# Second block's output projection: the attention half of its input turned early, first halves of all four tiles run around the recurrence's head norm

## What is computed

```python
def mixer_ab(h, w_in, lb, hg_norm, w_out):
    ...
    o_a = stick_breaking_attention(qa.reshape(sb_shape), ka.reshape(sb_shape), va.reshape(sb_shape))
    o_a = o_a.astype(h.dtype).reshape(B, S, SB_WIDTH)
    o_b = hgrn2(qb.reshape(B, S, HG_HEADS, HG_DK), fb.reshape(B, S, HG_HEADS, HG_DK), ib.reshape(B, S, HG_HEADS, HG_DV), lb)
    o_b = rmsnorm_2(o_b.astype(h.dtype), hg_norm) * jax.nn.silu(gb.reshape(B, S, HG_HEADS, HG_DV))
    o_b = o_b.reshape(B, S, HG_V)
    return jnp.concatenate([o_a, o_b], axis=-1) @ w_out
...
            h = h + mixer_ab(hn, ab_w_in[j], lower_bounds[j], hg_out_norm[j], ab_w_out[j])
...
        h = h + conv_glu_ffn(rmsnorm_2(h, ffn_norm[i]), ffn_up[i], ffn_conv[i], ffn_conv_b[i], ffn_down[i])
```

## Time and profile before

| | before |
|---|---|
| median of 3 runs (lowest to highest) | 1537.84 us (1537.67 to 1540.51) |
| span of the profiled execution | 1536.3 us |
| its own time with what lies around the span | not given apart; the median is 1.5 us over the span |
| TensorE busy | 1381.1 us (90%) |
| VectorE busy | 1029.5 us (67%) |
| ScalarE busy | 710.5 us (46%) |
| GpSimd busy | 568.9 us (37%) |
| mean granted TensorE clock | 0.973 |

### The profile page before, as it was taken

How to read it: one execution, slowest core, us unless ns; L and a number is a source line. 1 busy time by engine, 2 the same in 40 slices (tenths; PEclk the granted TensorE clock), 3 DMA queues, 4 the chain that set the end, 5 groups by cost and what they waited for, 6 DMA issues and landing times.

```text
span 1536.3 us, 18265 instructions
## 1 busy us (share of the span) xinstructions
PE 1381.1 (90%) x6001; PEld 969.0 (63%) x6001; DVE 1029.5 (67%) x1917; ACT 710.5 (46%) x1377; POOL 568.9 (37%) x541
## 2 busy tenths in 40 slices
PE   7999998778777887777779999999999999999998
PEld 6887963323333333333336878788888778888887
DVE  4885787666666666666655548659863686498734
ACT  5545453222333332233324463477645655776534
POOL 3040454333333333333344422055433512364414
PEclk9999999998998999999899999999999999999999
DMA  9295699999999999999998510567665443476650
GB/s 315 91 179 189 247 385 422 421 421 422 422 421 422 420 423 422 421 422 422 422 421 312 192 48 13 165 184 203 191 216 194 158 140 92 134 207 195 214 188 28
DMA packets 180739, 414.99 MB, mean 270 GB/s; under 512 B 9178, under 2 KB 113218, under 8 KB 148418
## 3 DMA queue, kind: packets, MB, share of 16 engines
q0 software_dynamic: 37440, 268.45, 42.1%
q1 hardware_dynamic: 143090, 145.66, 30.9%
q10 hardware_dynamic: 144, 0.04, 0.0%
HBM read 409.93 MB, written 4.19 MB: 270 GB/s over the span
## 4 chain that ended last, share of the span: by engine, by line
PE 52%; DMA 23%; DVE 9%; ACT 6%; POOL 5%; issue 4%; ACTq 0%; POOLq 0%; DVEq 0%
DMA expert_rows<-in_peer_uv,route_idx 13%; PE ps L2522 10%; DMA work_b<-in_peer_uv,route_idx 9%; PE ps L2347 8%; PE ps L2063 8%; PE ps L2065 8%; PE ps L2064 8%; PE ps L2523 5%; POOL weights_lo L588 2%; POOL expert_rows L637 2%; ACT weights_hi L433 2%; DVE weights_lo L440 2%; PE ps L2028 1%; DVE expert_rows L1645 1%; POOL ple_proj_lo L588 1%
## 5 line engine op out<-in xcount | busy, mean ns | idle before, releaser
L1645 DVE CUSTOM_DVE_ANT_0 expert_rows<-expert_rows,ps 128x1024 f32<-128x1024 f32 x180 | 219.4, 1220 | 133.9 <-DMA expert_rows<-in_peer_uv,route_idx 132.0
L2347 PE MATMUL ps<-expert_rows,proj 128*128 128x512 f32 x512 | 248.6, 644 | 63.5 <-ACT proj L952 63.5
L637 POOL DMA_INDIRECT expert_rows<-in_peer_uv,route_idx x191 | 184.5, 966 | 288.9 <-PE ps L2347 218.9
L588 POOL TENSOR_TENSOR weights_lo<-weights_raw,weights_hi 128x512 fp32r<-128x512 f32 x116 | 153.4, 1356 | 352.2 <-ACT weights_hi L433 310.3
L433 ACT CAST weights_hi<-weights_raw 128x2048 fp32r<-128x2048 f32 x98 | 185.5, 1917 | 106.3 <-PE ps L2065 82.6
L2347 PEld LDWEIGHTS ps<-expert_rows,proj 128*128 128x128 f32 x512 | 102.9, 206 | 208.4 <-issue 122.5
L2522 PE MATMUL ps<-x_normT,weights_hi 128*128 128x512 f32 x640 | 222.5, 393 | 0.0
L440 DVE TENSOR_TENSOR weights_lo<-weights_raw,weights_hi 128x2048 fp32r<-128x2048 f32 x69 | 163.1, 2370 | 61.2 <-ACT weights_hi L433 60.8
L938 ACT ACTIVATE proj<-proj 128x4 f32<-128x4 f32 x64 | 13.1, 205 | 408.0 <-DVE proj L1645 408.0
L2063 PE MATMUL ps<-weights_hi,x_normT 128*128 128x512 f32 (+1 forms) x496 | 188.2, 379 | 9.3 <-DVE weights_lo L440 3.2
L2065 PE MATMUL ps<-weights_hi,x_normT 128*128 128x512 f32 (+1 forms) x496 | 184.7, 372 | 0.0
(11 more groups left out here) (369 smaller groups left out, 2411.3 us busy)
## 6 DMA issues: line engine op xcount, KB each, us to landing
weights_raw<-in_ffn_up SPq DMA_DIRECT2D x88, 512.0 KB, 5.0
weights_raw<-in_ffn_down SPq DMA_DIRECT2D x22, 1024.0 KB, 5.0
weights_raw<-in_ab_w_in SPq DMA_DIRECT2D x14, 1024.0 KB, 5.1
weights_raw<-in_w_in SPq DMA_DIRECT2D x12, 1024.0 KB, 7.9
weights_raw<-in_ple_gate SPq DMA_DIRECT2D x8, 1024.0 KB, 6.3
weights_raw<-in_c_w_in SPq DMA_DIRECT2D x6, 1024.0 KB, 5.7
weights_raw<-in_w_out SPq DMA_DIRECT2D x4, 1024.0 KB, 12.0
weights_raw<-in_peer_w_query SPq DMA_DIRECT2D x4, 1024.0 KB, 11.9
```

The source lines that it names most:

```text
L588: ins = pool.tensor_tensor(w.lo[:, c], w.raw[:, c], w.hi[:, c].bitcast(F32), ALU.subtract)
L637: nc.gpsimd.indirect_dma_start(out=dst, out_offset=None, in_=table, in_offset=bass.IndirectOffsetOnAxis(ap=r_idx[:, q, n:n + 1], axis=0)). ...
L1645: ins = nc.vector.tensor_tensor_reduce(out=rows, in0=rows, in1=tokens, scale=1.0, scalar=0.0, op0=ALU.mult, op1=ALU.add, accum_out=r_dot[: ...
L2347: ins = pe.matmul(PS[:, (J[f"peer_{t}"] + m) % 8, :], DIAG[b][:, k, :], rows[:, m * BANK:(m + 1) * BANK], start=False, stop=False, skip_gr ...
```

## The change

- The attention half of `x_norm` is turned early: two jobs `mix1a`, between the first `spans` job and level 0, where a filler stood. ScalarE writes their high parts behind the exponentials of level 3's span (once the masked keys are done, whose place they take), VectorE the low parts behind the operands of level 1. The recurrence half follows as `mix1b` behind the head norm.
- TensorE runs the first halves of tiles (0,0) and (1,0) behind the outputs `hg_O`, turns the recurrence half, and runs the first halves of (0,1) and (1,1), then the four second halves in the old order. Fillers around them go.
- Pieces 1 and 2 of `about` change slots (0 and 2 lie in slots 0 and 1, 3 and 1 in slots 2 and 3), with new waits for the loads of 1 and 3.
- Splits: pieces 0 and 2 are cast on ScalarE ahead of the span exponentials; piece 0's low part is made on VectorE between the two copies of `sb_O`, piece 2's on GpSimd behind the masked keys. Piece 1 is cast behind the gate's silu, with its low part on VectorE where piece 0's was; piece 3 is cast behind `hg_O`, with its low part behind the low parts of `mix1b`.
- The head norm's rows, the squares and one level's operands move to other buffers.

```diff
-        ("sb_O", 2), ("hg_D", 2), ("hg_R3", 2), ("hg_L0", 2), ("hg_L1", 2), ...
+        ("sb_O", 2), ("hg_D", 2), ("hg_R3", 2), ("mix1a", 2), ("hg_L0", 2), ("hg_L1", 2), ...
-        ("mix1", 4), ("about", 3), ("norm3_0", 2), ("about_last", 1), ...
+        ("mix1b", 2), ("about", 3), ("norm3_0", 2), ("about_last", 1), ...
-        PIECES += [x for n in range(2) for x in chunk("about", n, ((0, 1), (2, 3))[n], a["ab_w_out_2"][0], 512 * n)]
+        PIECES += [x for n in range(2) for x in chunk("about", n, ((0, 3), (1, 2))[n], a["ab_w_out_2"][0], 512 * n)]
...
@@ SyncE
-            for p in halves(0):
+            for p in (0, 2):
                 load("about", p)
-            sp.wait_ge(pe_done, END["hg_L5"])
+            sp.wait_ge(pe_done, END["hg_L1"])
+            load("about", 1)
+            sp.wait_ge(pe_done, END["hg_L3"])
+            sp.wait_ge(sem("h_lev"), 12)
             sp.wait_ge(sem("h_bexp"), 1)
-            for p in halves(1):
-                load("about", p)
+            load("about", 3)
...
@@ GpSimd
             chunk_keys(hKST, hSF, 512, hKK)
-
+            split("about", 2)
             pool.wait_ge(sem("h_silu"), 2)
...
@@ ScalarE
+            for p in (0, 2):
+                split("about", p)
             for n in range(3, 6):
...
+                if n == 3:
+                    act.wait_ge(sem("kst_ready"), 6)
+                    x_hi(J["mix1a"], jobs=(0, 1))
             act.wait_ge(evac_done, END["ab_6b"])
             nc.scalar.activation(hg, hg, ACT.Silu).then_inc(sem("h_silu"), 1)
-            for p in halves(0):
-                split("about", p)
-            mixed(1, "about")
+            act.wait_ge(pe_done, END["hg_U"])
+            act.wait_ge(sem("h_lev"), 12)
+            split("about", 1)
+            sqrt_table()
+            act.wait_ge(pe_done, END["hg_O"])
+            split("about", 3)
+            root(SS[:, 16:24], SS[:, 8:16], GDV)
+            x_hi(J["mix1b"], pairs=PAIRS[2:], jobs=(0, 1))
...
@@ VectorE
             for t in range(TT):
                 j = J["sb_O"] + t
                 freed(nc.vector.tensor_copy(XN[:, t, 0:512], bank(j)), j)
+                if t == 0:
+                    split_lo(v, "about", 0)
...
             operands(0)
             operands(1)
+            x_lo(J["mix1a"], pairs=PAIRS[:2])
             mask_level(0)
...
             v.sem_inc(sem("state_ready"))
-            split_lo(v, "about", 0)
+            split_lo(v, "about", 1)
             v.wait_ge(sem("gates_gained"), 2 * TT)
-            head_norm(J["hg_O"], hg, XN[:, :, 512:1024], lambda: split_lo(v, "about", 1))
-            x_lo(J["mix1"])
-            for p in halves(1):
-                split_lo(v, "about", p)
+            head_norm(J["hg_O"], hg, XN[:, :, 512:1024], hOUTN, hSQ)
+            x_lo(J["mix1b"], pairs=PAIRS[2:])
+            split_lo(v, "about", 3)
...
@@ TensorE
             spans(3)
-            spin(J["hg_L0"], 4)
+            pe.wait_ge(evac_done, END["sb_O"])
+            mixed_T(J["mix1a"], PAIRS[:2])
             for n in range(2):
                 level(n)
...
-            mixed_T(1, END["sb_O"], 2)
-            spin(J["about"], 3)
...
-            residual_dense("about", 3, (END["mix1"], None), lambda: up_tokens(0, 0, 0), behind_norm=lambda: up_tokens(0, 1, 0))
+            dense_tile("about", 0, 0, (END["mix1a"], None), parts=(0,))
+            dense_tile("about", 1, 0, parts=(0,))
+            pe.wait_ge(sem("mixed"), TT * 2)
+            mixed_T(J["mix1b"], PAIRS[2:])
+            dense_tile("about", 0, 1, parts=(0,))
+            dense_tile("about", 1, 1, parts=(0,))
+            dense_tile("about", 0, 0, (None, END["mix1b"]), parts=(1,))
+            dense_tile("about", 1, 0, parts=(1,))
+            dense_tile("about", 0, 1, parts=(1,))
+            norm_T(3, 0)
+            dense_tile("about", 1, 1, parts=(1,))
+            up_tokens(0, 0, 0)
+            norm_T(3, 1)
+            up_tokens(0, 1, 0)
```

More of the change, by code:

```diff
@@ L41 @@
         ("ab_4", 2), ("ab_5", 1), ("sb_C", 6), ("ab_5b", 1), ("ab_6", 1), ("hg_B", 2), ("hg_T", 4), ("ab_6b", 1), ("hg_suf", 2),
[1 row of a table removed]
[1 row of a table added]
         ("hg_R5", 2), ("hg_L4", 2), ("hg_L5", 2),
         ("hg_O", 2),
-        ("mix1", 4), ("about", 3), ("norm3_0", 2), ("about_last", 1), ("norm3_1", 2), ("up0", 2 * FT),
+        ("mix1b", 2), ("about", 3), ("norm3_0", 2), ("about_last", 1), ("norm3_1", 2), ("up0", 2 * FT),
         ("down0_0", 2), ("norm4_0", 2), ("down0_1", 2), ("pT0", 1), ("gate0_first", 1), ("norm4_1", 2), ("gate0_mid", 1),
@@ L314, in build @@
         hE2 = M2[:, 1024:2048]
-        hE = (hE0, hE1, hE2, hBT, B[:, 2048:3072], A[:, 0:1024])
+        hE = (hE0, hE1, hE2, hBT, B[:, 0:1024], A[:, 0:1024])
+        hOUTN, hSQ = (A[:, n * 1024:(n + 1) * 1024].rearrange("p (t n) -> p t n", t=TT) for n in (1, 2))
         SPANS = SCR[:, 2048:2048 + 3 * P].rearrange("p (l t) -> p l t", l=3)
@@ L886, in mixed @@
                 sqrt_table()
[L887 to L891, removed]
-                    for p in halves(1):
[L893 to L897, removed]
+                root(SS[:, 16:24], SS[:, 8:16], GDV)
+                x_hi(J[f"mix{k}"], MIX_COL[k], MIX_PAIRS[k])
+                for p in halves(1):
+                    split(second, p)
             def residual_norm(k, name, between):
@@ L1423, in moba_queries, with head_norm @@
                 moba_qk(0, waiting=queries_splits)
-            def head_norm(first_job, gates, dst, between=None):
+            def head_norm(first_job, gates, dst, rows=OUTN, squares=SQ):
                 for t in range(TT):
[L1428 to L1433, removed]
+                    freed(nc.vector.tensor_copy(rows[:, t], bank(first_job + t)), first_job + t, True)
+                    step(nc.vector.tensor_tensor(squares[:, t], rows[:, t], rows[:, t], ALU.mult), wait=(t == 1))
+                step(nc.vector.tensor_reduce(SS[:, 8:16], squares.rearrange("p t (h n) -> p (t h) n", n=GDV), AX, ALU.add), "sumsq_ready")
+                step(nc.vector.tensor_tensor(rows, rows, gates, ALU.mult))
                 reciprocal_root(SS[:, 16:24], SS[:, 16:24])
                 for t in range(TT):
-                    o4, d4 = (x[:, t].rearrange("p (h n) -> p h n", n=GDV) for x in (OUTN, dst))
+                    o4, d4 = (x[:, t].rearrange("p (h n) -> p h n", n=GDV) for x in (rows, dst))
                     step(nc.vector.tensor_tensor(d4, o4, bc(SS[:, 16 + 4 * t:20 + 4 * t], GDV), ALU.mult), "mixed", t == 1)
@@ L2029, in transposes, with mixed_T @@
                 ins.then_inc(pe_done, 1)
-            def mixed_T(k, attended, recurrences):
-                if k:
-                    pe.wait_ge(evac_done, attended)
-                for n, m in enumerate(MIX_PAIRS[k]):
-                    if n == (2 if k else 0) and recurrences:
-                        if k:
-                            spin(J[f"mix{k}"] + n, 9)
-                        pe.wait_ge(sem("mixed"), TT * recurrences)
-                    if k == 0 and n == 2:
-                        pe.wait_ge(evac_done, attended)
-                    transposes(J[f"mix{k}"] + n, [XN[:, t, (2 * m + c) * P:(2 * m + c + 1) * P] for c in range(2) for t in range(TT)])
+            def mixed_T(j, pairs):
+                for n, m in enumerate(pairs):
+                    transposes(j + n, [XN[:, t, (2 * m + c) * P:(2 * m + c + 1) * P] for c in range(2) for t in range(TT)])
             xn_no = [0, 0]
@@ L2265, in _ @@
             spin(J["mix0"], 3)
-            mixed_T(0, END["mb_O1"], 1)
+            pe.wait_ge(sem("mixed"), TT)
+            mixed_T(J["mix0"], PAIRS[:2])
+            pe.wait_ge(evac_done, END["mb_O1"])
+            mixed_T(J["mix0"] + 2, PAIRS[2:])
             spin(J["wout"], 3)
```

1 line of the change is left out of this document (removed), and 2 rows, old and new, of the table PLAN.

## The result

Over 20 runs each, the changed kernel takes 1542.63 us (median; 1540.28 to 1546.91) and the kernel before 1540.26 us (1537.44 to 1547.75). The ratio is 1.0019, with a 95% interval of 1.0011 to 1.0028: 1.7 to 4.3 us slower. On the 1537.84 us from which the prediction counted, that is 1540.8 us; the forecast was 1537.9 and the range ended at 1540.4.

What follows compares the result with a forecast made beforehand. It took the dependency chain that starts TensorE's nearly gapless run behind 1004 us as the bound: delay 5.3 less gain 5.2 is +0.1 us on 1537.84, so 1537.9 us; 8-in-10 range 1534.3 to 1540.4.

Steps and rivals of the forecast that it cites:

- D: Delay with which the recurrence's outputs end, all from VectorE work ahead of or in the levels; forecast 5.3 us.
- The moved split of piece 0: On VectorE between the two copies of the attention's output; forecast to delay by 0.7 us, 1.1 with GpSimd's wait.
- The operand products: VectorE operands of levels 0 and 1, held up by GpSimd's keys and split of piece 2; 0.3 + 3.2 us.
- The low parts of the early turn: Two VectorE subtractions from PSUM for the half of the rows turned early; forecast +1.3 us.
- Waits: VectorE's waits at the first and third masked copies would shrink or go, giving back 0.6 us.
- What the change gives: First half tiles run inside the head norm, so the normed rows' transposes start sooner; gain 5.2 us less D.
- the half rate: TensorE's clock falling after the new 3.2 us idle before the up-projection; 1.4 us a stretch, left out of the main forecast.
- rival 3's second case: Half rate also catches the recurrence's outputs and following halves: 1.4 to 3 us more, 1540.9 to 1542; rival 3's chance 0.12.
- rival 1: VectorE keeps each level's operand pair together against GpSimd: D 3.0, 2.2 us gained, 1535.6; chance 0.20.
- rival 2: GpSimd's split of piece 2 is hidden: D 1.4 to 1.8, 3.4 to 3.8 us gained; chance 0.26.
- rival 4: The projection's first halves wait for weights, so the change does not do what it says; chance none.

Runs made afterwards that it cites:

- E2: Changed kernel, with GpSimd's split of piece 2 waiting for level 3's operands; ratio to the kernel before 1.0004.
- E4: Kernel before, with piece 1 cast ahead of the span exponentials and split on GpSimd behind the masked keys, VectorE's split of it removed; ratio to before 1.0023.
- E6: Changed kernel with the edits of E2 and E5 together; ratio to the kernel before 0.9987.
- E1: The changed kernel run again without any edit; ratio to the kernel before 1.0024.
- E5: Changed kernel, with VectorE's low part of piece 0 moved behind the last level and piece 1's behind mix1b's low parts; ratio to before 1.0030.
- E3: Changed kernel plus 12 fillers ahead of the up-projection, which proved too long; ratio to the kernel before 1.0018.
- E7: E6 plus 21 fillers: 12 ahead of the up-projection, 5 ahead of level 5, 4 ahead of the outputs; ratio to the kernel before 1.0009.
- E12: Changed kernel plus 11 fillers: 6 ahead of the up-projection, 3 ahead of level 5, 2 ahead of the outputs; ratio to the kernel before 1.0002.
- E9: Changed kernel plus 6 fillers ahead of the up-projection; ratio to the kernel before 1.0006.
- E10: E6 plus 6 fillers ahead of the up-projection; 1535.34 us, ratio to the kernel before 0.9977.
- E11: E10 plus 3 fillers ahead of level 5 and 2 ahead of the outputs; 1536.27 us, ratio to the kernel before 0.9976.

## Why the prediction was wrong

**What D costs: right, term by term.** D was put at 5.3; the outputs are 5.3 us late. The moved split of piece 0 makes the operands start 0.95 us later (0.7 to 1.1 forecast). The operand products take 6.1 us instead of 2.6, 3.5 more (0.3 + 3.2 forecast); E2 takes 3.1 of that away and E4 brings 3.7 into the old kernel. The low parts of the early turn take 1.4 us (1.3). Waits gave back about 0.5 (0.6). The Trainium skill, "SBUF — State Buffer", section "Who interferes with whom", has two-input VectorE products and GpSimd reads shut each other out for whole instructions; the products of 1.64 to 1.76 us, against 0.69 and with splits of 1.26, agree. So does its exception for one SBUF input: E2's split took 4.97 us beside such operations.

**What the change gives: right.** The first halves fit, the head norm's second copy starts 0.1 us behind the outputs instead of 0.6, the rows are turned 20.7 us behind them (20.6 forecast, 25.8 before). Gain less delay is +0.2 at the first turn (+0.1 forecast).

**The step that failed: the half rate, which the sum left out.** The idle of 3.07 us ahead of the up-projection was forecast (3.2), and so was its price, "half of its length, 1.4 us"; it cost 1.55 us between the two turns (2.4 in E6). What was wrong is the chance. From the earlier trace rows, where one such idle lowered the clock and another did not, I took the stretch as something that happens "at times", and forecast 1537.9 without it, 1539.3 with it. In all five profiles of kernels that leave this idle as it is (changed, E1, E2, E5, E6), the clock fell; in the seven with fillers in it (E3, E7 to E12), it stayed at 1.00 there. With 6 fillers and nothing else (E9) the changed kernel was then as fast as before as far as can be told, as the sum without the stretch had it.

The Trainium skill, "TensorE: Matmul & The Clock Gate", section "HAM oscillation — how this bites in real kernels", describes a kernel in which a wait of some 3 to 5 us ahead of each burst of matmuls brings half rate back every time. Here the idle of 3.07 us, at the short end of that, did so in five profiles of five, which agrees; forecast by that rule, the time would have been the 1539.3 us that the prediction gave as its second value.

**What the stretch does not explain.** The sum with the stretch as measured is 1537.84 + 0.2 + 1.6 = 1539.6 us, still inside the range; by the ratio the time was 1540.8. Of the rest, 0.36 us has its place. In a later norm VectorE's reciprocal starts 0.79 us behind what it waited for, instead of 0.43; so it does in all 12 profiles with the change, and neither in the kernel before nor in E4, which has the old code. The sum had no such term, and the cause is open. Timelines of VectorE, before and changed:

```profile
1230.17 0.18 DVE L1231 RECIPROCAL stats<-stats 128x4 f32<-128x4 f32 x1 [0.43 <-ACT stats L745]
...
1233.60 0.18 DVE L1237 RECIPROCAL stats<-stats 128x4 f32<-128x4 f32 x1 [0.79 <-ACT stats L748]
```

That makes 1540.0 us, inside the interval (1539.5 to 1542.1). The last 0.8 us is not shown. It can be scatter, the offset ahead of the stage (E1), or half rate at the outputs in other executions. The last is rival 3's second case, which E3 and E10 show to happen, at 4.2 us (first turn of E3 against the changed kernel, and of E10 against E11; 1.4 to 3 forecast, which makes 1540.7 to 1542.3 by its own terms, not 1540.9 to 1542). Neither of the changed kernel's two profiles has it.

**The base was low.** 1537.84 was a median of three runs; 20 gave 1540.26. This doesn't touch the ratio, but in absolute time the changed kernel's 1542.63 us is 2.2 us above the range's end, not 0.4.

**The other rivals.** VectorE did not keep its operand pairs together (rival 1), the split was not hidden (rival 2), and the first halves waited for no weights (rival 4).

## What to carry to other kernels

GpSimd work that reads SBUF should not stand beside VectorE products of two SBUF tensors on the critical path: put it where VectorE reads PSUM (here this alone was worth 2.9 us). When a move takes TensorE off the path, look at the idle that it leaves just ahead of the next run: here 3.07 us of it cost a half-rate start each time unless fillers covered it, and fillers are to be measured, since too many cost what they were to save. And an experiment whose time doesn't fit, here the three with long fillers, is first to be read in its own timeline.

## What the runs showed of the hardware that was not expected

**The order in which VectorE and GpSimd take turns is not settled by who comes first.** In the feed-forward layer a VectorE split of 2.29 us begins 0.33 us behind the first of four GpSimd split operations, in E5 and E6 alike. Timelines of E5, VectorE, GpSimd and TensorE:

```profile
1193.85 6.83 DVE L441 TENSOR_TENSOR weights_lo<-weights_raw,weights_hi 128x2048 fp32r<-128x2048 f32 x1 [0.40 <-ACT weights_hi L434]
...
1193.52 5.01 POOL L591 TENSOR_TENSOR ple_proj_lo<-ple_proj_raw,ple_proj_hi 128x512 fp32r<-128x512 f32 x4
...
1200.73 0.50 PE L2060 MATMUL ps<-weights_hi,x_normT 128*128 128x512 f32 x1 [2.96 <-DVE weights_lo L441]
```

And of E6, VectorE and GpSimd:

```profile
1192.05 3.10 DVE L441 TENSOR_TENSOR weights_lo<-weights_raw,weights_hi 128x2048 fp32r<-128x2048 f32 x1 [0.40 <-ACT weights_hi L434]
...
1191.72 7.08 POOL L591 TENSOR_TENSOR ple_proj_lo<-ple_proj_raw,ple_proj_hi 128x512 fp32r<-128x512 f32 x4
```

In E6 VectorE waited for one GpSimd operation and then had its turn; in E5 (and E7) it waited for all four, and TensorE stood still for 2.96 us. Both kernels are the same there. E5's profile lost 3.2 us by it, E7's 4.4, where the clock fell behind the idle. This is 2 of 14 profiles; how much of the scatter of the times it makes is not shown.

**Half rate can last long behind short idles.** E10's 10 us came behind two idles of 1.56 and 1.23 us; in E6, whose code is the same up to there, idles of 1.57 and 1.22 us left the clock at 1.00. Six profiles have this pair (1.38 to 1.57 us, then 1.22 to 1.24): the clock fell in E3 and E10, and stayed in the changed kernel, E2, E6 and E9.
